# Attention heads with the values stationary and the probabilities scaled before their transposes

## The reference, cut to what matters

```
s = q @ k.T * hd ** -0.5              # 64 channels per head, masked
p = softmax(s)                        # banded heads: with one sink logit in the sum
o = p @ v                             # 256 tokens x 64 channels
y = concat(o of all heads) @ w_out    # 1024 x 1024
```

## Time and profile before

| what | value |
|---|---|
| median of 3 runs | 1097.64 us (1095.02 to 1100.95) |
| the profiled execution | 1100.35 us, span 1098.5 us |
| PE busy | 1005.2 us, 92% of the span |
| DVE busy | 721.7 us, 66% |
| ACT busy | 539.8 us, 49% |
| mean granted TensorE clock | 0.951 |

### The profile page before, as it was taken

One profiled execution on the slowest core, in us unless ns is written; L12 is line 12 of the kernel. 1 busy time (PEld: TensorE's weight loads), 2 busy tenths in 40 slices (PEclk: granted clock), 3 DMA queues, 4 the chain that ended last, 5 costly groups with the idle time before them and its releaser, 6 DMA issues.

```text
span 1098.5 us, 14738 instructions
## 1 busy us (share of the span) xinstructions
PE 1005.2 (92%) x5742; PEld 827.4 (75%) x5742; DVE 721.7 (66%) x1105; ACT 539.8 (49%) x859; POOL 60.4 (6%) x47
## 2 busy tenths in 40 slices
PE   4798798999999989999899999988999899988895
PEld 2484477989898866777798989866787777767784
DVE  2477658877776676555885554586455587884475
ACT  2355354654463154554454546345656476637472
POOL 0000000500000000000150000000000000110000
PEclk8798699999998889999999999999999899998998
DMA  9766446879896467332688865535343155540040
GB/s 329 281 209 224 150 144 209 274 264 332 304 327 245 144 236 267 118 114 77 198 286 246 244 192 176 196 109 179 119 143 123 49 192 178 183 157 20 30 153 38
DMA packets 105303, 204.85 MB, mean 186 GB/s; under 512 B 3834, under 2 KB 38100, under 8 KB 105236
## 3 DMA queue, kind: packets, MB, share of 16 engines
q1 hardware_dynamic: 102180, 193.25, 52.0%
q0 software_dynamic: 3056, 10.67, 3.6%
HBM read 202.76 MB, written 1.15 MB: 186 GB/s over the span
## 4 chain that ended last, share of the span: by engine, by line
PE 69%; DVE 17%; ACT 6%; DMA 4%; issue 4%; SPq 1%; DVEq 0%; ACTq 0%
PE bank L1545 13%; PE bank L1547 13%; PE bank L1546 13%; PE bank L1599 5%; PE bank L1600 5%; PE bank L1601 5%; DVE w_lo L1699 4%; PE bank L1658 4%; DMA raw<-in_ada_w 3%; PE bank L1620 3%; PE bank L1640 2%; ACT w_hi L1220 2%; PE bank L1448 1%; ACT probs L1400 1%; DMA raw<-in_mlp_w 1%
## 5 line engine op out<-in xcount | busy, mean ns | idle before, releaser
L1699 DVE TENSOR_TENSOR w_lo<-raw,w_hi 128x2048 fp32r<-128x2048 f32 (+2 forms) x134 | 309.4, 2317 | 163.0 <-ACT w_hi L1220 161.9
L1220 ACT ACTIVATE w_hi<-raw 128x2048 fp32r<-128x2048 f32 (+2 forms) x134 | 248.2, 1856 | 132.9 <-PE bank L1547 86.1
L1545 PE MATMUL bank<-w_lo,ht_hi 128*128 128x512 f32 (+1 forms) x544 | 220.8, 406 | 14.9 <-issue 4.0
L1547 PE MATMUL bank<-w_hi,ht_lo 128*128 128x512 f32 (+1 forms) x528 | 207.8, 394 | 0.0
L1546 PE MATMUL bank<-w_hi,ht_hi 128*128 128x512 f32 (+1 forms) x528 | 207.5, 393 | 0.0
L1545 PEld LDWEIGHTS bank<-w_lo,ht_hi 128*128 128x128 f32 x544 | 105.1, 193 | 42.0 <-issue 16.8
L1599 PE MATMUL bank<-ht_hi,w_lo 128*128 128x256 f32 x448 | 127.5, 285 | 1.3 <-DVE w_lo L1699 1.3
L1600 PE MATMUL bank<-ht_lo,w_hi 128*128 128x256 f32 x448 | 126.7, 283 | 0.0
L1601 PE MATMUL bank<-ht_hi,w_hi 128*128 128x256 f32 x448 | 126.7, 283 | 0.0
L1547 PEld LDWEIGHTS bank<-w_hi,ht_lo 128*128 128x128 f32 x528 | 101.4, 192 | 22.0
L1546 PEld LDWEIGHTS bank<-w_hi,ht_hi 128*128 128x128 f32 x528 | 102.2, 194 | 19.5 <-issue 0.2
(11 more groups left out here) (222 smaller groups left out, 1327.2 us busy)
## 6 DMA issues: line engine op xcount, KB each, us to landing
raw<-in_mlp_w SPq DMA_DIRECT2D x64, 1024.0 KB, 6.0
raw<-in_ada_w SPq DMA_DIRECT2D x48, 1024.0 KB, 5.1
raw<-in_a_w_in SPq DMA_DIRECT2D x16, 1024.0 KB, 5.3
raw<-in_c_w_in SPq DMA_DIRECT2D x12, 1024.0 KB, 5.5
raw<-in_b_w_in SPq DMA_DIRECT2D x10, 1024.0 KB, 5.0
raw<-in_ple_w_gate SPq DMA_DIRECT2D x8, 1024.0 KB, 5.0
raw<-in_ab_w_in SPq DMA_DIRECT2D x4, 1024.0 KB, 11.0
raw<-in_ab_w_out SPq DMA_DIRECT2D x4, 1024.0 KB, 5.2
```

The lines of the kernel that those rows point to most:

```text
L1220: nc.scalar.activation(split_parts(n)[0], raw_tile(t), ACT.Copy).then_inc(high_done, 1)
L1545: nc.tensor.matmul(dst, a_hi[:, c, rows], lo[:, k, :], start=it["first"] and k == 0, stop=False)
L1547: mm = nc.tensor.matmul(dst, a_lo[:, c, rows], hi[:, k, :], start=False, stop=it["last"] and k == it["kc"] - 1)
L1699: nc.vector.tensor_tensor(lo, raw_tile(split[n]), hi.bitcast(F32), ALU.subtract).then_inc(low_done, 1)
```

## The change

For the banded, sparse and causal modes (`TURNED_OUT`), three things differ. The probabilities are scaled by the inverse sums in place before they are transposed, by DVE for the sparse and causal heads and by ACT for the banded ones; the inverse sums are DVE's in all. In `values` the 64 value columns are stationary, on one half of the array's columns per head, and `probs_t` is moving, 256 and then 128 columns, so that the result stands channel by token; ACT copies it to `out_turned`, a view of `u`. `split_rows` for these outputs becomes `split_out`, in the same places of the plan, which takes high and low parts straight from `out_turned`; PE has no share in it. In `split_out`, ACT and DVE wait for the last projection that reads `ht` and for ACT's copy of the last pair. The other modes keep their code.

```diff
+TURNED_OUT = ("window", "sparse", "causal")
+NORMED_BY_SCALAR = ("window",)
...
+    def split_out(half, last):
+        if half == 0:
+            projected[0] = max(i["tile"] for i in plan if i["kind"] == "tokens" and i["lhs"] == "ht")
+        add("split_out", a=4 * half, after=evicted(last), projected=projected[0], high=tick("high"))
+        tick("cut", 2)
+        cuts["ht"] = (count["cut"] if half == 0 else cuts["ht"][0], count["cut"])
...
-    split_rows("o", KD, "ht", 0, halves=(0,), after=evicted(o_last))     # four such calls
+    split_out(0, o_last)
...
         @block.scalar
+                elif kind == "split_out":
+                    act.wait_ge(tile_done, it["projected"] + 1)
+                    for b, used in it["after"]:
+                        act.wait_ge(bank_free[b], used)
+                    a = it["a"]
+                    nc.scalar.activation(ht_hi[:, a:a + 2, :], out_turned[:, a:a + 2, :], ACT.Copy).then_inc(high_copied, 1)
+                elif kind == "values" and it["mode"] in TURNED_OUT:
+                    b, _ = it["banks"][0]
+                    act.wait_ge(head_out, 2 * it["g"] + 2)
+                    nc.scalar.activation(out_turned[:, it["heads"][0][4] // 2, :], bank[b][:, 0:S], ACT.Copy).then_inc(bank_free[b], 1)
                 elif kind == "probs":
                     g = it["g"]
+                    if it["mode"] in NORMED_BY_SCALAR:
+                        act.wait_ge(sums_turned, g + 1)
+                        for j in range(2):
+                            for t in range(T):
+                                rows = probs[:, g % 2, j, t, 0:head_cols(it["mode"], t)]
+                                ins = nc.scalar.activation(rows, rows, ACT.Copy, scale=rs[:, g % PAIRS_HELD, t, j:j + 1])
+                            ins.then_inc(normed, 1)
...
         @block.tensor, probs
+                        elif mode in TURNED_OUT:
+                            pe.wait_ge(normed, 2 * g + j + 1)
...
         @block.tensor, values
+                        for k in range(T):
+                            t0 = next(t for t in range(T) if (k, t) in blocks)
+                            i = blocks.index((k, t0))
+                            for j in range(2):
+                                v = it["heads"][j][3]
+                                mm = nc.tensor.matmul(bank[b][j * HD:(j + 1) * HD, t0 * P:T * P], tok[:, k, v:v + HD],
+                                                      probs_t[:, j, i:i + T - t0, :].rearrange("p b s -> p (b s)"),
+                                                      start=k == 0, stop=k == T - 1)
...
         @block.vector
+                elif kind == "split_out":
+                    dve.wait_ge(tile_done, it["projected"] + 1)
+                    for b, used in it["after"]:
+                        dve.wait_ge(bank_free[b], used)
+                    a = it["a"]
+                    link(nc.vector.tensor_copy(ht_hi[:, a + 2:a + 4, :], out_turned[:, a + 2:a + 4, :]))
+                    low_part(ht_lo[:, a + 2:a + 4, :], out_turned[:, a + 2:a + 4, :], ht_hi[:, a + 2:a + 4, :])
+                    dve.wait_ge(high_copied, it["high"])
+                    low_part(ht_lo[:, a:a + 2, :], out_turned[:, a:a + 2, :], ht_hi[:, a:a + 2, :])
+                elif kind == "probs" and it["mode"] in TURNED_OUT:
+                    for b, used in it["scores"]:
+                        dve.wait_ge(bank_free[b], used + 1)
+                    if mode == "window":
+                        link(nc.vector.tensor_tensor(sums[:, r, :, :], sums[:, r, :, :], sink_exp[:, r, :, :], ALU.add))
+                    nc.vector.reciprocal(rs[:, r, :, :], sums[:, r, :, :]).then_inc(sums_turned, 1)
+                    if mode in NORMED_BY_SCALAR:
+                        continue
+                    dve.wait_ge(sums_turned, g + 1)
+                    for j in range(2):
+                        for t in range(T):
+                            rows = probs[:, g % 2, j, t, 0:head_cols(mode, t)]
+                            ins = nc.vector.tensor_scalar(rows, rows, rs[:, r, t, j:j + 1], None, ALU.mult)
+                        ins.then_inc(normed, 1)
```

More of the change, by code:

```diff
@@ L251, in split_rows @@
             cuts[dst] = (count["cut"] if a == 0 else cuts[dst][0], count["cut"])
+    def split_out(half, last):
[4 more added lines that the diff above has]
+        cuts["ht"] = (count["cut"] if half == 0 else cuts["ht"][0], count["cut"])
+    projected = [0]
     def gate_row(s, pairs=None):
@@ L596, in make_plan @@
     y[1](0, 1, ts=(0,), look=4)
-    split_rows("o", KD, "ht", 0, halves=(1,), after=evicted(o_last))
+    split_out(1, o_last)
     y[1](0, 2, ts=(1,))
@@ L646, in make_plan @@
     scores(4, [turned[4]])
-    split_rows("o", KD, "ht", 0, halves=(0,), after=evicted(o_last))
+    split_out(0, o_last)
     turn_pair(6, (q1, k1), qk_rows)
@@ L897, in block_kernel @@
         sums = sb("sums", [P, PAIRS_HELD, T, 2])
-        rs = sb("rs", [P, T, 2])
+        rs = sb("rs", [P, PAIRS_HELD, T, 2])
         sink_exp = sb("sink_exp", [P, PAIRS_HELD, T, 2])
@@ L985, in block_kernel @@
         head_out = sem("head_out")
+        sums_turned = sem("sums_turned")
+        normed = sem("normed")
         gate_done = sem("gate_done")
@@ L1021, in source @@
             return sources[it["src"]][:, t, c * P:(c + 1) * P]
+        out_turned = u[:, :, :].rearrange("p t d -> p (t d)").rearrange("p (c s) -> p c s", c=KD)
         def sums_of(it):
@@ L1648, in _ @@
                     b, _ = it["banks"][0]
+                    if mode in TURNED_OUT:
+                        for s, used in it["turned"]:
+                            pe.wait_ge(bank_free[s], used)
+                        for k in range(T):
[6 more added lines that the diff above has]
+                                                      start=k == 0, stop=k == T - 1)
+                                if k == T - 1:
+                                    mm.then_inc(head_out, 1)
+                        continue
                     for j in range(2):
@@ L2150, in _ @@
                             .then_inc(band_ready, 1)
-                elif kind == "values":
+                elif kind == "split_out":
[8 more added lines that the diff above has]
+                elif kind == "probs" and it["mode"] in TURNED_OUT:
+                    mode, g = it["mode"], it["g"]
+                    r = g % PAIRS_HELD
+                    for b, used in it["scores"]:
[4 more added lines that the diff above has]
+                    if mode in NORMED_BY_SCALAR:
+                        continue
+                    dve.wait_ge(sums_turned, g + 1)
[4 more added lines that the diff above has]
+                        ins.then_inc(normed, 1)
+                elif kind == "values" and it["mode"] not in TURNED_OUT:
                     mode, g = it["mode"], it["g"]
@@ L2156, in _ @@
                     hh = it["heads"][0][4]
-                    if mode == "window":
-                        link(nc.vector.tensor_tensor(sums[:, r, :, :], sums[:, r, :, :], sink_exp[:, r, :, :], ALU.add))
-                    link(nc.vector.reciprocal(rs[:, :, :], sums[:, r, :, :]))
+                    link(nc.vector.reciprocal(rs[:, r, :, :], sums[:, r, :, :]))
                     dve.wait_ge(head_out, 2 * g + 2)
@@ L2162, in _ @@
                     nc.vector.tensor_tensor(o, bank[b][:, 0:T * P].rearrange("p (t h d) -> p t h d", t=T, h=2),
-                                            rs[:, :, :].unsqueeze(3).broadcast_to([P, T, 2, HD]), ALU.mult).then_inc(bank_free[b], 1)
+                                            rs[:, r, :, :].unsqueeze(3).broadcast_to([P, T, 2, HD]), ALU.mult).then_inc(bank_free[b], 1)
                     dve.wait_ge(bank_free[b], used + 1)
```

## The result

The changed kernel takes 1114.62 us (median of 4 runs, 1111.16 to 1118.31) where before takes 1098.01 (median of 4). The ratio is 1.0163, 95% interval 1.0135 to 1.0191: 16.6 us slower. The forecast was 1103.5 (+5.9), in a range of 1095 to 1111: the direction was right, the size a third of what came.

The account below looks back on a forecast made before the run. PE was taken as ending most steps, with DVE's queue the bound in the banded heads. Causal layer +2.4 and layer 0 +3.5 gave +5.9 us, 1103.5 on the median of 1097.64, range 1095 to 1111.

Parts of the forecast that it names:

- The values item: PE's values items: two column halves take 0.95 us instead of 1.34, a gain of 0.39, ends 0.75 and 1.26.
- The single waits in the causal layer: PE's transposes wait for DVE's scales: 2.0 us at pairs 0, 4; 0.9 at 1, 2, 5, 6; 0.5 at 3.
- The tail: Causal layer's end: `y_ln` 7.5 us behind the last values' matmuls instead of 10.1, a gain of 2.6.
- +8.1, less 8 x 0.39 = 3.1: Causal layer: waits for scales add 8.1 us, eight cheaper values items save 3.1; with the tail's 2.6 off, +2.4.
- the clock takes more: Rival: PE idles in new places and the sparse stretch runs at half clock: +4 more, 1108 us; chance 0.20.
- I take 4.8 for the first sparse scores: Banded heads: ACT's scales delay scores and DVE's mask, so the first sparse scores start 4.8 us late, ends 2.6 and 6.
- PE's own share: Banded heads: PE's pair 3 work, scaled only behind the top-k rounds, can be later than the mask's 3.5 to 4.9 us.
- The scale and transposes then end at 151.4, against 149.8: +1.6: Sparse heads, pair 7: DVE's scale queues behind a weight split ending at 149.9, so the transposes end 1.6 us later.
- The forecast for the end of `probs(4)`: Sparse heads: from first sparse scores to the end of `probs(4)` 12.7 us instead of 13.7, so -1.0.
- my own second sign of being wrong: The prediction is wrong if the clock comes out at full where it was at half.
- DVE's scales hide: Rival: PE reaches the transposes late anyway, so only gains remain, about 11 us at best, 1087 us; chance 0.10.

Follow-up runs that it names:

- Experiment 3: The changed kernel with idle bf16 mask products put into PE's waits for the scales, nothing moved: 1108.0 us, ratio 1.012 to the kernel before.
- Experiment 9: The changed kernel with only the sparse pairs' scales moved ahead, banded and causal heads left as changed: 1105.9 us, ratio 1.008 to the kernel before.
- experiment 4: The changed kernel with DVE's causal sums, reciprocals and scales ahead of the next pair's reductions, layer 0 left as changed: 1107.6 us, ratio 1.010.
- experiment 5: The changed kernel with every pair's sum, reciprocal and scale in an item of its own, placed earlier in the queues: 1085.9 us, ratio 0.989.
- experiment 8: The changed kernel with only the banded heads taken back to the old code, sparse and causal left as changed: 1114.8 us, ratio 1.017.
- experiment 10: The kernel before, with only 32 idle bf16 products added in PE's wait for the top-k mask: 1091.4 us, ratio 0.9954.
- experiments 1: The changed kernel without any scale or wait for it, outputs by channel kept and not divided by their sums: 1082.7 us, ratio 0.987.
- experiment 2: The changed kernel with the scale ahead of the transposes kept, but old twelve-pass outputs, DVE's plain copy and PE's turns: 1159.4 us, ratio 1.058.

## Why the prediction was right or wrong

**The values item.** Forecast 0.95 for 1.34, ends 0.75 and 1.26. Measured 0.80 from start to start at full clock (497.86 to 498.66), that is the 0.65 of streaming and 0.15 for all the rest: the two halves run beside each other and the 0.2 of overhead is paid once at most. The gain was 0.54, where I had 0.39. The rule of the Trainium skill (TensorEngine Tiling (Array Packing), Key Properties) that a change of mode drains the engine didn't show as a cost here; by it the saving could have vanished, and 0.54 of 1.34 was saved.

**The single waits in the causal layer: right.** Forecast 2.0 at pairs 0 and 4, 0.9 at 1, 2, 5 and 6, 0.5 at 3 and 0 at 7, in all 8.1. Measured 1.95, 1.15, 0.40 and 0, in all 8.9. The tail, too: `y_ln` stands 7.5 behind the last values, as forecast.

**The failed step of the causal layer** is the sum itself: "+8.1, less 8 x 0.39 = 3.1", and then the tail. It has no term for the clock. With the measured terms, 8.9 for the waits, 8 x 0.54 = 4.3 and 2.6 off, 2.4 became 2.0; the half clock adds 4.6 of lost work and makes it 6.6, against 7.8 measured. Most of the last 1.2 is small change: a values item in front of a wait takes its whole 0.87 and not 0.80 (five times), the mask 0.28 and not 0.12 (twice), and PE's wait for exponentials is 2.06 for 1.25 + 0.50. I had seen the clock fall in layer 0 and priced it there, in the rival "the clock takes more", as one event of 4 us. The causal layer had none, and I didn't ask whether my own new waits would make some. The trace before had the warning in it: the half clock that I read at 98 to 101 follows a wait of only 1.82 us.

```profile
96.84 2.50 PE L1658 MATMUL bank<-tok,probs_t 128*128 128x64 f32 x12 [1.82 <-ACT probs_t L1412]
```

**The failed step of the banded heads** is "I take 4.8 for the first sparse scores", which goes by DVE's mask. The mask was late by just that (ready at 126.85, 5.1 later), and `scores(3)` started at 109.50, 0.4 past my upper end. But PE's own share, named in the sentence before and not priced, came 3.5 later than the mask: it turned pair 2 only at 118.72, behind ACT's scale, and ran at half clock until 128. Experiment 3 gives the split: with the clock held up for most of the way, the start is 4.3 late, and so about 4 of the 8.4 is clock, to the microsecond by which the start itself varies. The Trainium skill (TensorE: Matmul & The Clock Gate, What's actually happening) has the rate follow how busy PE has been recently, and reports two ratios for it, half and full. The rows agree with the two ratios, 0.50 and 1.00; the values between are means over a window that holds both.

**The failed step of the sparse heads** is "The scale and transposes then end at 151.4, against 149.8: +1.6", with 1.2 taken off again up to the last values. The wait is 2.40. What it lacked is the half clock behind it, over the columns (1.71 for 0.95), the gate row (3.75 for 1.95) and the first matmuls of the projection, and that behind `probs(4)`. The forecast for the end of `probs(4)` was right for its stretch (12.55 for 12.7), but I stopped there, and the fit is in part luck: I had the scores at half clock, and they ran at full. That was my own second sign of being wrong, the clock at full where it was at half. At the end of `probs(4)` the clock was at half again, where before had just come back to full. This stage made +5.6 for +0.4. Experiment 9 shows that it is these two waits and what follows them, 9 us in the times.

**The order of the causes.** From after, the causal scales ahead give 6.5 us by the ratios (experiment 4; 9.6 in the trace), the sparse ones 9 (experiment 9), and all together 29 (experiment 5). So the banded ones are worth some 14 if the parts add there, with the sparse scales ahead, where taking the banded heads back gave nothing while the sparse scales were late (experiment 8); a version with the banded scales alone ahead was not run. That is why no single experiment but the one with all scales ahead gives the loss back. How much of each wait's price is idle time and how much clock was separated by experiments 3 and 10 in the traces, to a microsecond or two; the times alone don't give it.

**The rival "DVE's scales hide"** gave 1087 as its best case. Experiment 5 reaches 1085.9 with the same work on the same engines. The price was in the place in the queue and the clock behind it, not in the work.

## What to carry to other kernels

When an operation moves ahead of a consumer, put it in its engine's queue at the place where its inputs are ready, not where the consumer's item happens to stand: in queues served in order, the same scales in another place moved the kernel by 29 us. Price a new idle stretch on PE with the clock behind it, at every place, and look at whether a clock that was at half before will now be at full and the reverse. If PE must wait for a long time before dense work, idle products in the wait are worth a trial; here they gave 0.5% to the kernel before, by 32 instructions.

## What the runs showed of the hardware

- The clock can fall behind waits that I thought short: 1.82 us before, and one of 1.95 us in the causal layer after, and 2.06 us in experiments 1, 4 and 5, each had PE at half for 3 to 7 us. Waits of 1.15 us in the same layer and of 1.40 in experiment 4 did not.
- The length of a single wait does not settle it. A wait of 2.17 us for DVE's low part of `ht`, just behind the causal layer, had the clock fall behind it before (at 534.1) and left it at 1.00 in experiments 1 and 5 (until the traces' 522 and 536 at least). After the 2.06 us in the kernel after, it stayed at 1.00 for 2.4 us and fell in the next wait. What decides between them no run here isolates.
- Fed with bf16 products of a mask for 5.4 us of a wait of some 6, PE kept 2.4 GHz through it (experiment 10); their results are overwritten.
- A values item on two column halves lasts 0.87 us at full clock and 1.55 at half; the twelve-pass item lasts 1.45 to 1.55 and 2.79 (the last in experiment 2).
- In-place scales by a factor per row from SBUF take 1.01 us for four pieces of 128 and 256 columns on DVE, 1.49 on ACT.
